# The border of time mix and scan: gates kept in SBUF, gate weights loaded earlier, the last stores issued in the scan, residual reloaded in the output stage

## The reference, cut to what matters

```
r, k, v = mixes of x times w_rkv          w, a = low-rank functions of x
g  = sigmoid(xg @ g1) @ g2                             # the gates
kk = k*k_k / |k*k_k|;   k = k*(1 + (a-1)*k_a);   decay = exp(-exp(w))
S  = S*decay + (S @ -kk) (kk*a)^T + v k^T;   y = S @ r     # the scan
yn = group_norm(y)*ln_w + ln_b
bonus = sum(r*k*r_k) * v                               # sum over the head
h  = h + ((yn + bonus) * g) @ w_o
```

## Time and profile before

| | us |
|---|---|
| median of 3 runs | 3958.17 |
| lowest, highest | 3956.24, 3964.32 |
| profiled execution, its time | 3958.94 |
| span of the profiled execution | 3957.1 |
| TimeMixIn, last part (k loop from m = 2, gates, last stores) | 1505 to 1650 |
| rwkv_scan | 1650.7 to 2089 |
| TimeMixOut | 2089 to about 2230 |

### The profile page before, as it was taken

One profiled execution on the slowest core, in us unless ns is written; L12 is line 12 of the kernel. 1 busy time (PEld: TensorE's weight loads), 2 busy tenths in 40 slices (PEclk: granted clock), 3 DMA queues, 4 the chain that ended last, 5 costly groups with the idle time before them and its releaser, 6 DMA issues. The chain is left out here.

```text
span 3957.1 us, 62731 instructions
## 1 busy us (share of the span) xinstructions
PE 3622.7 (92%) x27516; PEld 2953.5 (75%) x27516; DVE 2518.4 (64%) x2223; ACT 1537.1 (39%) x1634; POOL 1172.5 (30%) x537
## 2 busy tenths in 40 slices
PE   8999999999989998677776999999998999998897
PEld 6778788878767776577774788887876888875675
DVE  5564766687756848444545566768867888827532
ACT  5563433344534348544335523344444222113412
POOL 1135455455412111233220455455531000000211
PEclk9999999999999999899998999999999999998998
DMA  2112223254122336612113033344312222222422
GB/s 96 48 38 67 80 96 109 94 195 146 60 84 75 125 103 194 226 63 92 60 41 133 27 105 106 104 159 152 115 53 92 75 80 80 80 110 54 151 99 101
DMA packets 189360, 392.48 MB, mean 99 GB/s; under 512 B 16208, under 2 KB 85072, under 8 KB 183312
## 3 DMA queue, kind: packets, MB, share of 16 engines
q1 hardware_dynamic: 150368, 311.91, 23.9%
q10 hardware_dynamic: 38720, 76.56, 5.2%
HBM read 277.79 MB, written 110.10 MB: 98 GB/s over the span
## 5 line engine op out<-in xcount | busy, mean ns | idle before, releaser
L3710 POOL MEMSET ssm_toep<- 128x4096 f32 x1 | 3.5, 3511 | 544.5 <-POOLq L3409 544.5
L3296 DVE SCALAR_TENSOR_TENSOR H<-hy_cu,par,H 128x1024 f32<-128x1024 f32 x120 | 153.3, 1277 | 0.0
L269 POOL TENSOR_TENSOR wlo1C<-fast_raw,whi1C 128x1024 fp32r<-128x1024 f32 (+1 forms) x40 | 112.5, 2812 | 112.1 <-ACT whi1C L259 112.1
L269 POOL TENSOR_TENSOR wlo0B<-fast_raw,whi0B 128x1024 fp32r<-128x1024 f32 (+1 forms) x40 | 112.9, 2824 | 107.6 <-ACT whi0B L259 107.6
L3296 DVE SCALAR_TENSOR_TENSOR hy_odd<-hy_cu,par,hy_odd 128x1024 f32<-128x1024 f32 x112 | 143.0, 1277 | 0.0
L269 POOL TENSOR_TENSOR wlo1A<-fast_raw,whi1A 128x1024 fp32r<-128x1024 f32 (+1 forms) x40 | 111.4, 2786 | 103.7 <-ACT whi1A L259 103.7
L269 POOL TENSOR_TENSOR wlo1B<-fast_raw,whi1B 128x1024 fp32r<-128x1024 f32 (+1 forms) x39 | 108.0, 2768 | 113.6 <-ACT whi1B L259 113.6
L1007 DVE TENSOR_TENSOR fast_xl<-fast_xr,fast_xh 128x2048 fp32r<-128x2048 f32 (+1 forms) x42 | 127.7, 3062 | 21.3 <-ACT fast_xh L848 21.3
L269 POOL TENSOR_TENSOR wlo0A<-fast_raw,whi0A 128x1024 fp32r<-128x1024 f32 (+1 forms) x40 | 109.1, 2727 | 104.9 <-ACT whi0A L259 104.9
L269 POOL TENSOR_TENSOR wlo0C<-fast_raw,whi0C 128x1024 fp32r<-128x1024 f32 (+1 forms) x39 | 108.0, 2770 | 104.3 <-ACT whi0C L259 104.3
L942 DVE TENSOR_TENSOR fast_g<-fast_g,flow_rms 128x1024 f32<-128x1024 f32 x44 | 128.6, 2923 | 1.5
(11 more groups left out here) (1448 smaller groups left out, 12074.8 us busy)
## 6 DMA issues: line engine op xcount, KB each, us to landing
fast_raw<-ffn_in_dram SPq DMA_DIRECT2D x88, 512.0 KB, 4.0
fast_xr<-ffn_x SPq DMA_DIRECT2D x28, 1024.0 KB, 6.0
sc_ops<-rw_arbkv SPq DMA_DIRECT2D x15, 1280.0 KB, 6.3
fast_raw<-ffn_out_dram SPq DMA_DIRECT2D x32, 512.0 KB, 3.7
wraw1A<-hybrid_in_dram SPq DMA_DIRECT2D x24, 512.0 KB, 3.5
wraw1B<-hybrid_in_dram SPq DMA_DIRECT2D x24, 512.0 KB, 3.5
ffn_x<-fast_g ACTq DMA_DIRECT2D x22, 512.0 KB, 3.3
ffn_x<-fast_e ACTq DMA_DIRECT2D x22, 512.0 KB, 2.8
```

Source lines behind the costliest of these rows:

```text
L269: eng.tensor_tensor(self.slot(wlo, n), self.raw[n], self.slot(whi, n).bitcast(fp32), ALU.subtract)\
L3296: op = dve.scalar_tensor_tensor(out=acc, in0=c[:, j:j + T], scalar=w, in1=acc, op0=ALU.mult, op1=ALU.add)
```

## The change

Nothing of the arithmetic changes. What moves:

1. **Gates in SBUF.** The eight gate tiles are copied by ACT into the room of H (`gates_kept`) and stay there until TimeMixOut. The eight stores to `rwd_g` and its eight loads are gone. rr and vv move to H's second half; for m = 7 they have places of their own (`rr7`, `vv7`). Gates 4 to 7 take the places of rr and vv and wait for the stores from there.
2. **Gate weights early.** Both strips of `rw_g2` are loaded by the k loop's last turn, ahead of the store of m = 5.
3. **Late last stores.** For m = 7 only the four pieces for the scan's first pair are copied in TimeMixIn. Its five full stores stand at the start of the scan's SP queue (`store_last`), followed by the wait for all stores.
4. **DVE order.** The norm's bank is read right behind the running sums (`run_sums`); for m = 7 `finish(6)` comes ahead of the rest of `before(7)`, and the bonus of m = 7 is last.
5. **PE order.** The head sum of m = 7 moves into the middle of `gates(1)`, and the banks are given out to match.
6. **H reloaded later.** The eight reloads of H move from pair 3 of the scan to TimeMixOut; each waits until the gate tile in its place has been used. DVE waits for them at the first and the fifth addition to H. The weight loads of w_o strips 2 and 3 move ahead of the fourth bonus load.

```diff
@@ TimeMixIn, plan
                     self.at["g", j] = n
-                    self.g_turns += [W.turn_of[n], W.extra(), W.extra(), W.extra()]
+                    self.g_turns += [W.turn_of[n], W.extra()]
+                    if j == 1:
+                        self.rk_turn.append(W.extra())
+                    self.g_turns += [W.extra(), W.extra()]
@@ TimeMixIn, SP
+                def store_last(sp):
+                    m = DT - 1
+                    sp.dma_start(by_pair(m, 1), in_pairs(r_tile(m))).then_inc(*tick("op_out_rr_1", 16))
+                    for name, j in (("ks", 0), ("aa", 2), ("ab", 3)):
+                        sp.dma_start(by_pair(m, j), in_pairs(L[name](m % 2))).then_inc(*tick(f"op_out_{name}_1", 16))
+                    sp.dma_start(in_pairs(BN[m, :, :]), in_pairs(v_tile(m))).then_inc(*tick("op_out_vv_1", 16))
+                scan.store_last = store_last
...
                     for m in range(2, DT):
-                        W.load(sp, at["sa", m] + (2 if m < DT - 1 else 0))
+                        W.load(sp, at["sa", m] + 2)
                         store(m - 2)
                         load_v(m)
-                    W.load(sp, at["g", 1])
                     scan_first()
                     store(DT - 2)
-                    store(DT - 1)
+                    store_first_pair(DT - 1)
@@ TimeMixIn, PE
                         for i in range(4):
+                            if j == 1 and i == 2:
+                                key_sum(DT - 1)
                             self.part(pe, n, self.g_turns[4 * j + i], [2 * i, 2 * i + 1], self.g, "w_mm" if i == 3 else "g_mm")
@@ TimeMixIn, ACT
-                        if j >= 3:
-                            act.wait_ge(*after(f"tm_g_out_{j % 3}", 16 * (j // 3)))
+                        if j >= 4:
+                            act.wait_ge(*(after("op_out_vv_1", 48), after("op_out_rr_1", 48), after("op_out_vv_0", 64), after("op_out_rr_0", 80))[j - 4])
                         act.wait_ge(*(after("g_mm", 3 * (j // 4) + j % 4 + 1) if j % 4 < 3 else after("w_mm", n + 1)))
-                        act.activation(g_stage[:, j % 3, :], W.flat(turn), ACT.Copy).then_inc(*W.out(turn))
-                        act.wait_ge(*W.freed(turn))
-                        act.dma_start(in_pairs(G_[j, :, :]), in_pairs(g_stage[:, j % 3, :])).then_inc(*tick(f"tm_g_out_{j % 3}", 16))
+                        act.activation(gates_kept[j], W.flat(turn), ACT.Copy).then_inc(*W.out(turn))
@@ TimeMixIn, DVE
-                    before(0)
-                    before(1)
+                    for m in range(2):
+                        run_sums(m)
+                        before(m)
                     finish(0)
...
                         bonus(m - 1)
-                        before(m)
-                        finish(m - 1)
+                        run_sums(m)
+                        if m < DT - 1:
+                            before(m)
+                            finish(m - 1)
+                        else:
+                            finish(m - 1)
+                            before(m)
+                    finish(DT - 1)
                     bonus(DT - 1)
-                    finish(DT - 1)
@@ rwkv_scan, SP
-                    for name in KEPT[0:13]:
+                    room.store_last(sp)
+                    for name in KEPT[0:10]:
                         sp.wait_ge(*after(name, 0))
...
-                        if p == 3:
-                            for m in range(DT):
-                                sp.dma_start(H[:, m, :], HS_[m, :, :]).then_inc(*tick("h_back", 16))
@@ TimeMixOut, SP
+                    def back(k):
+                        sp.wait_ge(*after("ro_gated", k + 1))
+                        m = GATE_AT[k]
+                        sp.dma_start(H[:, m, :], HS_[m, :, :]).then_inc(*tick("h_back_a" if k < 6 else "h_back_b", 16))
...
                     for k in range(1, DT):
                         load(k)
-                    W.load(sp, at[3])
+                        if k == 2:
+                            W.load(sp, at[3])
+                        if k >= 4:
+                            back(k - 4)
+                    for k in range(4, DT):
+                        back(k)
@@ TimeMixOut, DVE
                         dve.wait_ge(*after("w_mm", n + 1))
+                        if m == 0:
+                            dve.wait_ge(*after("h_back_a", 16 * 6))
+                        if m == 4:
+                            dve.wait_ge(*after("h_back_b", 16 * 2))
```

98 lines of the change are left out of this document (60 added, 38 removed).

## The result

| | median, us | lowest to highest | runs |
|---|---|---|---|
| kernel before | 3959.41 | 3956.24 to 3964.32 | 4 |
| changed kernel | 3936.59 | 3932.74 to 3937.32 | 4 |

The ratio is 0.9937, 95% interval 0.9924 to 0.9949: 25 us (20 to 30) off a kernel of 3959. The forecast was 3930.0, range 3922 to 3941. The profiled execution of the changed kernel is the fastest of its four (3932.74, span 3931.0), so a bare subtraction of the two traces, 26.1 us, is some 3 us too kind. PE's busy time is 3622.7 us with 27516 products, as in the earlier trace rows, in a shorter span.

What follows compares the result with a forecast made beforehand. PE, busy 92% of the span, was taken as the bound, with time to gain only where it stands still. Terms -23.6 - 1.2 + 1.5 - 3.9 - 1.0 = -28.2 us gave 3930.0 us, range 3922 to 3941.

Steps and rivals of the forecast that it cites:

- Border, -23.6: From the k loop's end to the scan: the scan's first product comes at 1627.05 instead of 1650.67, 23.6 us earlier.
- this wait ends, the next one is PE's gates: Border: with the gate weights early, PE does the gates without a gap from 1602.3, the last parts ending at 1625.4.
- The gain in the k loop: k loop: reading the norm's bank earlier removes PE's two waits for DVE's bonus, 0.78 and 0.89 us, 1.7 us in all.
- rival C: Border: the store of ab of m = 5 lands 9.8 us after issue, replacing the old wait; +6, 3936.0; chance 0.08.
- Rival D: Border's end: SP's queue still ends the block, 12 transfers at 1.97 us each; +6.1, 3936.1; chance 0.08.
- Start of the scan, -1.2: Scan's first products: PE idles less beforehand, so its clock should still be 2.4 GHz; 1.2 us gained (0 to 2.6).
- Late stores, +1.5: First 10 us or so of the scan: five stores, 2.6 MB, run beside it and cost PE 1.5 us (0 to 4.6).
- Rival A: Scan's start: late stores starve PE, costing 4.6 us and the 1.2 clock gain; total -23.9, 3934.3; chance 0.12.
- H reload, -3.9: Scan, stretch of pair 3: transfers slow the scan, so moving the reload of H out gains 3.9 us (2.5 to 5.3).
- Output stage, -1.0: Output stage: ACT's 1.10 us wait for the second weight strip goes, reaching the first gated tile; 1.0 us gained (0 to 1.1).
- The likeliest case: Whole kernel: the forecast itself, all terms summed to -28.2 us, 3930.0 us; chance 0.58.
- Rival E: Scan: shifted loads drop PE's clock to 0.86 in all eight stretches, costing 35 us, slower than before; chance 0.02.

Runs made afterwards that it cites:

- b2: Kernel before, with only the raw gate weights issued early, ahead of the stores of m = 5: ratio 0.9976 to the kernel before.
- b3: Kernel before, with only the five whole stores of the last turn moved into the scan: ratio 0.9974 to the kernel before.
- a1: Changed kernel, with the gate weights issued late again, behind the store of m = 5: ratio 0.9952 to the kernel before.
- a3: Changed kernel, with DVE reading the norm's bank late again in turns m = 0 to 6: ratio 0.9934 to the kernel before.
- a4: Changed kernel, with the old order of the tail back on DVE and PE: ratio 0.9925 to the kernel before.
- c1: Changed kernel, with both the late read of the norm's bank and the old tail order back: ratio 0.9943 to the kernel before.
- d2: Changed kernel, with the five late operands stored a second time to a tensor nobody reads: ratio 0.9926 to the kernel before.
- d1: Changed kernel, with the second half of each operand load, from pair 2 on, held until the running pair's first state: ratio 0.9962 to the kernel before.

## Why the prediction was right, and where it was not

**Border, -23.6: measured -22.0.** The step "this wait ends, the next one is PE's gates" held, and each of the two waits had a price of its own: b2 and b3 give 9.9 and 8.7 us. Counted from the sums of m = 0, those of m = 7 came at 130.3 us (forecast 129.9), the gates at 129.4 (128.9) and the scan at 154.6 (153.6); the head sum and the two parts behind it took 7.3 us, not 6.8. That is 1.0 of the 1.6 us; the other 0.6 is scatter of before and after around the means. Two terms were too large. The gain in the k loop was put at 1.7 and was 1.2, of which m = 7 gave some back. It rested on two waits of PE, and I took all of both. And DVE's sums of m = 7 waited 3.65 us for ACT, which had to wait itself for a landing (0.87 us for k) that I had seen in the earlier trace rows and let vanish. The landing of ab of m = 5 came 1607.41 - 1601.64 = 5.8 us behind its issue, not 3.8: rival C in small, 1.05 us. Rival D did not come: 0.46 us for each of the last pieces.

**Start of the scan, -1.2: about right.** The first product took 1.10 us, and the first pair was 1.0 us shorter in the means of seven and six traces. What the sum did not have is that the full clock does not last: in after it was down to 0.50 in the second 10 us.

**Late stores, +1.5: they are free.** The failed step is the one that took the row of the reload as a bound for this place. That row is a late fetch of PE's instructions. In its first 15 us of the scan PE passed two ends of a block, some 3 and 12 to 13 us in, with no idle piece that lacks a releaser; there it waits for ACT's copies. Ten stores cost no more than five. Rival A is out.

**H reload, -3.9: right, -4.7.** The likes that I compared it with were scattered by 2 us each way; five against eight traces are clear. What I had not seen is that half of it comes by the clock, and that of the idle 4.57 us 1.2 to 1.8 stand there without the reload too. The means of the scan: 430.7 us in the five traces with everything moved (after, a1, a3, a4, c1), 435.2 in before and b2, which differ by 6.5, a gain of 4.5 us with an error of some 3, where the sum said 3.6 in this stage. The -9.7 between the first two traces was for the other half chance.

**Output stage, -1.0: not there.** The step that failed is "this chain leads to the first gated tile". The wait for the strip hid a wait for a bank of PE; take it away and the other shows, 1.00 us, and ACT is no earlier. Over eight traces with the new stage the mean is 84.8 us, over five with the old 83.8. Most traces of either kernel stand at one of two levels (83.5 to 84.3, and 85.2 to 85.3), and in the two read closely, after and a1, these go with the time at which the clock comes back. Windows of 5 us that begin 30 us behind the first product of the output stage, where the strips' products start, after and then a1_weights_late:

```profile
2089.44:2094.44 5.00, 5.00 (x13) 3.92 (x12) 4.96 (x5) 0.00 (x0) 0.00 (x0) 0.50 0.00 0
```
```profile
2096.43:2101.43 5.00, 5.00 (x17) 3.99 (x16) 4.96 (x5) 0.00 (x0) 0.00 (x0) 0.69 0.00 0
```

In the same 5 us PE did 13 of these instructions in after, at 1.2 GHz throughout, and 17 in a1, where the clock rose earlier. Whether the change has a part in the 0.9 us stays open; five and eight traces with such levels don't tell.

**The sum.** -22.0 - 4.5 + 0.9 = -25.6 us by the stages, and 25 (20 to 30) by the runs; I had said 28.2. The likeliest case held. Of the 6.6 us between 3930.0 and 3936.6, 2.6 are these terms (border 1.6, output 1.9, scan -0.9). The other 4.0 can't be told from scatter: the interval is 5 us to each side, and a3 and d2, no better by their stages, gave 3933.78 and 3928.70 on other chips.

**Rival E**, the one on the other side, did not happen to this change: its six whole stretches stand at 0.97 to 1.00. But its mechanism exists. d1 put the load halves apart and brought it about, with clocks of 0.91 to 0.95 over whole stretches and some 12 us lost.

## What to carry to other kernels

When two waits end a stage one behind the other on different engines, remove both: here each alone gave 9 to 10 us, and together with the rest of the change 22. Put transfers that nothing waits for where the compute engine is itself waiting for data (late stores at the scan's start were free, a reload in its midst cost 4.7 us), and do not split a crowd without measuring (d1). Where an engine runs many short instructions and stands idle with no semaphore to blame, count its instructions from piece to piece: equal blocks say that it waits for its own code. A stage's difference from one pair of traces is worth little under 3 us; untouched stages of every other run are free samples of the scatter.
